# Half-size products with weight sums on GpSimd in block 2's first mixer

## The reference, cut to what matters

```
h = rms_norm_2(x, norm_mix[l]) * (1.0 + sc1) + sh1
proj = h @ w_in[l]
dn_qkv, dn_z, dn_a, dn_b, sw_q, sw_k, sw_v, gate_a, gate_b = split(proj)
o_dn = gated_delta_rule_chunked(dq, dk, dv, g, beta)       # 8 heads of 128, chunks of 64
o_dn = rms_norm_2(o_dn, dn_norm[l]) * silu(dn_z)
y_a = o_dn @ w_dn_out[l]
y_b = swa_sink_attention(sq, sk, sv, swa_sinks[l]) @ w_swa_out[l]   # 16 heads of 64
x = x + gt1 * ((sigmoid(gate_a) * y_a + sigmoid(gate_b) * y_b) @ w_o[l])
```

## Time and profile before

| | us |
|---|---|
| median of three runs | 2584.17 (2582.35 to 2584.47) |
| the profiled execution | 2589.01 |
| its span, first to last instruction | 2587.2 |

### The profile page before, as it was taken

The page is one execution under the profiler, slowest core; times in us unless marked ns, Lnnn a source line. Parts: engine busy times, 40 slices in busy tenths (PEclk is TensorE's granted clock), DMA queues, the critical chain, the costliest instruction groups (busy, mean ns, idle before and its releaser), DMA issues.

```text
span 2587.2 us, 39719 instructions
## 1 busy us (share of the span) xinstructions
PE 2514.9 (97%) x16196; PEld 1938.5 (75%) x16196; DVE 1595.8 (62%) x3137; ACT 654.9 (25%) x1733; POOL 44.7 (2%) x84
## 2 busy tenths in 40 slices
PE   6999899999999999999999999999999999999999
PEld 2545557888888876599996845669997864668999
DVE  4857667655777645466663764447773664447785
ACT  3135422111101112122212153233321134232320
POOL 0000000000000001000000000000000000000000
PEclk9999999999999999999999999999999999999999
DMA  8531215555575758245644423135654333115653
GB/s 338 185 115 27 64 33 164 162 169 173 187 269 187 277 203 308 87 123 155 169 158 148 163 77 120 67 104 146 174 173 143 130 123 105 66 68 151 175 175 119
DMA packets 342646, 386.70 MB, mean 149 GB/s; under 512 B 8110, under 2 KB 285190, under 8 KB 330176
## 3 DMA queue, kind: packets, MB, share of 16 engines
q1 hardware_dynamic: 330896, 320.89, 39.3%
q0 software_dynamic: 8832, 57.26, 6.2%
q10 hardware_dynamic: 2736, 6.01, 0.6%
HBM read 383.08 MB, written 1.05 MB: 148 GB/s over the span
## 4 chain that ended last, share of the span: by engine, by line
PE 84%; DVE 7%; issue 3%; ACT 3%; DMA 3%; ACTq 0%; DVEq 0%; SPq 0%
PE acc L923 32%; PE mx L923 14%; PE acc L974 9%; PE acc L962 9%; PE acc L988 6%; PE acc L1402 2%; PE acc L1351 2%; PE mx L1756 1%; DMA ring<-in_odd_w_in 1%; PE mx L1213 1%; DVE arena L3574 1%; DVE hT L2683 1%; DMA mod_w<-in_w_ada 1%; PE mx L1743 1%; PE mx L1814 1%
## 5 line engine op out<-in xcount | busy, mean ns | idle before, releaser
L923 PE MATMUL acc<-arena 128*128 128x128 f32 (+1 forms) x2248 | 353.8, 300 | 1.0 <-ACT gate L2312 0.5
L923 PEld LDWEIGHTS acc<-arena 128*128 128x128 f32 x2248 | 310.0, 192 | 16.8 <-ACT gate L2312 0.9
L2651 DVE SCALAR_TENSOR_TENSOR arena<-mod_w,vcols,arena 128x2048 f32<-128x2048 f32 x98 | 228.3, 2347 | 59.4 <-DMA mod_w<-in_w_ada 45.2
L974 PE MATMUL acc<-hT,ring 128*128 128x256 f32 (+1 forms) x1024 | 250.0, 406 | 1.3 <-DVE arena L3351 0.8
L988 PE MATMUL acc<-ring,hT 128*128 128x512 f32 x512 | 247.4, 605 | 0.7 <-ACT hT L2095 0.7
L974 PEld LDWEIGHTS acc<-hT,ring 128*128 128x128 f32 x1024 | 193.9, 190 | 54.9 <-issue 29.4
L923 PE MATMUL acc<-hT,ring 128*128 128x128 f32 (+1 forms) x1368 | 206.1, 301 | 2.8 <-ACT hT L2062 1.4
L3027 DVE TENSOR_TENSOR arena<-ring 128x512 f32<-128x512 f32 (+1 forms) x136 | 91.6, 673 | 179.8 <-PE acc L923 174.4
L962 PE MATMUL acc<-ring,hT 128*128 128x512 f32 x448 | 195.5, 597 | 5.9 <-ACT hT L2062 4.6
L923 PEld LDWEIGHTS acc<-hT,ring 128*128 128x128 f32 x1368 | 184.8, 191 | 16.1 <-issue 6.4
L923 PE MATMUL acc<-arena,ring 128*128 128x128 f32 (+1 forms) x1256 | 194.2, 298 | 0.0
(11 more groups left out here) (472 smaller groups left out, 3531.3 us busy)
## 6 DMA issues: line engine op xcount, KB each, us to landing
ring<-in_w_in SPq DMA_DIRECT2D x28, 2048.0 KB
mod_w<-in_w_ada POOLq DMA_DIRECT2D x48, 1024.0 KB, 5.9
ring<-in_ffn_w_in SPq DMA_DIRECT2D x88, 512.0 KB
ring<-in_w_up SPq DMA_DIRECT2D x88, 512.0 KB
mod_w<-in_mod_w SPq DMA_DIRECT2D x36, 1024.0 KB, 4.9
ring<-in_odd_w_in SPq DMA_DIRECT2D x20, 1024.0 KB
ring<-in_ffn_w_out SPq DMA_DIRECT2D x16, 1024.0 KB
ring<-in_w_down SPq DMA_DIRECT2D x16, 1024.0 KB
```

The lines of the kernel that those rows point to most:

```text
L923: ins = nc.tensor.matmul(out, w[:, k, :], h[:, k, :], start=start and k == 0, stop=stop and k == n - 1, skip_group_check=more)
L974: ins = nc.tensor.matmul(b[:, 0:hi - lo], w[:, k, P * f:P * (f + 1)], hT[:, k, lo:hi], start=k == 0, stop=k == KD - 1)
L2651: ins = V.scalar_tensor_tensor(acc_, mod_w[:, i % 2, :], vcols[:, at:at + 1], acc_, ALU.mult, ALU.add)
```

## The change

The four large products of each layer become eight units, one for each weight tile of 512 columns (z, z, attention output twice, gate b twice, gate a twice). A unit is seven products of 128 tokens by 256 columns over 4 blocks of 128, 14 "halves" of two float32 matmuls each; `fill(n)` issues n halves. So a layer has 112 fills where it had 128. `pair_fills` gives one half instead of two at steps 4, 7, 11 and 15. The 8 and 8 fills around the norms become 6 and 6; the one between the two parts of inversion levels 1 to 4 goes; the six at the end of a head group become one ahead of the third ACT copy's wait and five at the end.

POOL computes the four weight sums of every unit (1024 columns each, in SBUF). Each waits for the one before it; the fourth also waits for product 2 of the unit (half 10), whose weights it overwrites, and product 3 (halves 13, 14) waits for the fourth. A ring slot is free when product 3 is done. DVE makes four input sums (512 columns each) for h and for the attention output in each layer, and three additions of 256 columns for each unit. ACT makes four copies of 256 columns for each unit, in place of two of 512.

Two smaller edits: DVE's three instructions for mask, maximum and shift become two `tensor_tensor_reduce`, one for each head, writing the negated scores and their minimum (ACT's exponential gets scale -1). In the first block's recurrence `scores` issues, for each 32 query columns of a chunk, a product with that chunk's 64 keys only, into its half of the partitions: 16 products of 64 x 32 in place of 8 of 128 x 64, for each head and direction.

```diff
+WIDE, HALVES = 8, 14
+WIDE_COPIES, WIDE_SUMS = (("p1", 2), ("u2", 6), ("u3", 9), ("c01", 12)), (("c11", 9), ("c00", 10), ("c10", 14))
 def pair_fills(step):
 
-    return 1 if step in (0, 1, 2, 9, 13, 16, 17) else 2 if step < PAIRS else 0
+    return 1 if step in (0, 1, 2, 4, 7, 9, 11, 13, 15, 16, 17) else 2 if step < PAIRS else 0
...
+            def wide_weights_summed(l, n):
+                u = wide_unit(l, n)
+                c = RV_TILES + WIDE * l + n
+                t = pl.tile[f"wide@{l}"] + 2 * n
+                b = rv_tile(t)
+                t3, t2 = wide_weight_sums(n)
+                if n == 0:
+                    need(pool, merged, 5 * l)
+                elif n == 1:
+                    pool.wait_ge(acc_full, pl.own[f"swa_qkT@{l}"][-1] + 1)
+                elif n == 5:
+                    pool.wait_ge(rv_z, wide_unit(l, 3) + 1)
+                elif n == 6:
+                    pool.wait_ge(rv_z, wide_unit(l, 3) + 1)
+                    pool.wait_ge(rv_p6, wide_unit(l, 5) + 1)
+                else:
+                    pool.wait_ge(rv_p7, u - 1)
+                    if n == 7:
+                        pool.wait_ge(rv_p6, u)
+                pool.wait_ge(w_in[t // 2 % RING], pl.landed[t][1])
+                nc.gpsimd.tensor_tensor(t3, b[0][0], b[0][1], ALU.subtract).then_inc(rv_t, 1)
+                pool.wait_ge(rv_t, 4 * c + 1)
+                nc.gpsimd.tensor_tensor(b[0][1], b[0][1], b[1][1], ALU.add).then_inc(rv_t, 1)
+                pool.wait_ge(rv_t, 4 * c + 2)
+                nc.gpsimd.tensor_tensor(t2, b[0][1], b[0][0], ALU.subtract).then_inc(rv_t, 1)
+                pool.wait_ge(rv_t, 4 * c + 3)
+                pool.wait_ge(rv_p2, u + 1)
+                nc.gpsimd.tensor_tensor(b[1][0], b[1][0], t2, ALU.subtract).then_inc(rv_t, 1)
+            for n in range(WIDE):
+                wide_weights_summed(0, n)
...
+                for n in range(WIDE):
+                    u, c = wide_unit(l, n), RV_TILES + WIDE * l + n
+                    summed_in = 4 * (2 + 2 * l + (n in (2, 3)))
+                    x_ = wide_x(n)
+                    a_, (s1, s2, s3, s4) = wide_inputs(n), wide_input_sums(n)
+                    t3, t2 = wide_weight_sums(n)
+                    if n < 2:
+                        bank_free(n)
+                    else:
+                        pe.wait_ge(rv_c01, u)
+                    first = tile.n
+                    weights(512)
+                    b = rv_tile(first)
+                    half(x_, a_[0][0], b[0][0], 0)
+                    yield
+                    half(x_, a_[0][0], b[0][0], 1).then_inc(rv_p1, 1)
+                    yield
+                    pe.wait_ge(rv_t, 4 * c + 2)
+                    pe.wait_ge(rv_s, summed_in + 1)
+                    if n == 0:
+                        bank_free(2)
+                    else:
+                        pe.wait_ge(rv_c10, u)
+                    half(wide_z, s1, b[0][1], 0)
+                    yield
+                    half(wide_z, s1, b[0][1], 1)
+                    yield
+                    pe.wait_ge(rv_t, 4 * c + 3)
+                    pe.wait_ge(rv_s, summed_in + 3)
+                    pe.wait_ge(rv_p1s, u + 1)
+                    half(x_, s2, t2, 0, first=False)
+                    yield
+                    half(x_, s2, t2, 1, first=False).then_inc(rv_p6, 1)
+                    yield
+                    if n == 0:
+                        bank_free(3)
+                    elif n == 1:
+                        emptied(pl.own[name_of("dn_cum")][0] + 1, "V")
+                    else:
+                        pe.wait_ge(rv_c00, u)
+                    half(wide_p2, a_[0][1], b[1][0], 0)
+                    yield
+                    pe.wait_ge(rv_u2s, u + 1)
+                    half(x_, s3, t3, 0, first=False)
+                    yield
+                    half(x_, s3, t3, 1, first=False).then_inc(rv_p7, 1)
+                    yield
+                    half(wide_p2, a_[0][1], b[1][0], 1).then_inc(rv_p2, 1)
+                    yield
+                    pe.wait_ge(rv_u3s, u + 1)
+                    pe.wait_ge(rv_s, summed_in + 4)
+                    half(x_, s4, b[1][1], 0, first=False)
+                    yield
+                    half(x_, s4, b[1][1], 1, first=False).then_inc(rv_x, 1)
+                    yield
+                    pe.wait_ge(rv_t, 4 * c + 4)
+                    pe.wait_ge(rv_c11, u + 1)
+                    half(wide_z, a_[1][1], b[1][0], 0, first=False)
+                    yield
+                    half(wide_z, a_[1][1], b[1][0], 1, first=False).then_inc(rv_z, 1)
+                    yield
+            def fill(n):
 
                 for _ in range(n):
-                    s = filling.next()
-                    k, i = s % KD, tiles[s // KD % 2]
-                    if s % 16 == 0:
-                        filling.w = weights(512)
-                    if k == 0:
-                        filling.b = bank()
-                    ins = nc.tensor.matmul(filling.b, src[:, k, P * i:P * (i + 1)], filling.w[:, k, :],
-                                           start=k == 0, stop=k == KD - 1)
-                    if k == KD - 1:
-                        ins.then_inc(acc_full, 1)
+                    next(filling.wide)
...
                 for t in range(NT):
-                    s = slice(P * t, P * (t + 1))
                     for early in (True, False):
                         at = 32 * (early == (d == 1))
-                        q = e_set[d][0][:, s].rearrange("p (n t) -> p n t", t=64)[:, :, at:at + 32]
-                        o = hg_bank(h, d, 1)[:, s].rearrange("p (n t) -> p n t", t=64)[:, :, at:at + 32]
-                        ins = nc.tensor.matmul(o, (h_kz[d] if early else e_set[d][1])[:, s], q, start=True, stop=True)
+                        for c in (2 * t, 2 * t + 1):
+                            half, s = slice(64 * (c % 2), 64 * (c % 2) + 64), slice(64 * c, 64 * c + 64)
+                            q = slice(64 * c + at, 64 * c + at + 32)
+                            ins = nc.tensor.matmul(hg_bank(h, d, 1)[half, q], (h_kz[d] if early else e_set[d][1])[:, s],
+                                                   e_set[d][0][:, q], start=True, stop=True)
                 ins.then_inc(hg_s, 1)
...
+                        if name == "p1":
+                            act.wait_ge(rv_p1, u + 1)
+                            act.wait_ge(rv_c00, u)
+                            nc.scalar.activation(wide_p1, wide_x(n), ACT.Copy).then_inc(rv_p1s, 1)
+                        elif name == "u2":
+                            act.wait_ge(rv_p6, u + 1)
+                            act.wait_ge(rv_c10, u)
+                            nc.scalar.activation(wide_u2, wide_x(n), ACT.Copy).then_inc(rv_u2s, 1)
+                        elif name == "u3":
+                            act.wait_ge(rv_p7, u + 1)
+                            act.wait_ge(rv_c11, u)
+                            nc.scalar.activation(wide_u3, wide_x(n), ACT.Copy).then_inc(rv_u3s, 1)
+                        else:
+                            act.wait_ge(rv_x, u + 1)
+                            nc.scalar.activation(wide_out(n, 0, 1), wide_x(n), ACT.Copy).then_inc(rv_c01, 1)
...
                 silu_tanh()
-                act.wait_ge(acc_a, pl.emptied("A", pl.own[name_of("dn_z")][3] + 1))
+                all_wide(2)
...
-                        link(V.scalar_tensor_tensor(S[:, :, 0:w], mx[:, 0:2, 0:w], HD ** -0.5, rep(mask(i), 1, [P, 2, w]),
-                                                    ALU.mult, ALU.add))
-                        link(V.reduce_max(st[:, 40 + c:42 + c], S[:, :, 0:w], AXX))
-                        V.scalar_tensor_tensor(st[:, 8 + c:10 + c], st[:, 40 + c:42 + c], -1.0, less[:, j, :],
-                                               ALU.mult, ALU.min).then_inc(att_m, 1)
+                        for v in range(2):
+                            ins = V.tensor_tensor_reduce(S[:, v, 0:w], mx[:, v, 0:w], mask(i), -HD ** -0.5, less[:, j, v:v + 1],
+                                                         ALU.add, ALU.min, st[:, 8 + c + v:9 + c + v])
+                        ins.then_inc(att_m, 1)
...
+                def wide_inputs_summed(n):
+                    (a00, a01), (a10, a11) = wide_inputs(n)
+                    s1, s2, s3, s4 = wide_input_sums(n)
+                    s0 = 4 * (2 + 2 * l + (n in (2, 3)))
+                    V.tensor_tensor(s1, a10, a00, ALU.subtract).then_inc(rv_s, 1)
+                    V.tensor_tensor(s3, a11, a10, ALU.subtract).then_inc(rv_s, 1)
+                    dve.wait_ge(rv_s, s0 + 1)
+                    V.tensor_tensor(s2, a11, s1, ALU.subtract).then_inc(rv_s, 1)
+                    dve.wait_ge(rv_s, s0 + 3)
+                    V.tensor_tensor(s4, a01, s2, ALU.subtract).then_inc(rv_s, 1)
+                halves_done = Cursor()
+                def wide_done(n):
+                    lo = halves_done.n
+                    halves_done.n += n
```

(69 more changed lines are left out.)

152 lines of the change are left out of this document (97 added, 55 removed).

## The result

| | us |
|---|---|
| changed kernel, median of four runs | 2651.7 (2647.1 to 2662.3) |
| kernel before, on the same chip | 2583.3 (2580.7 to 2584.5) |
| ratio | 1.0271, 95% interval 1.0251 to 1.029 |

The change makes the kernel 68 us slower. The forecast was 2569, its range ended at 2618, and its likeliest case had the wrong sign.

The account below looks back on a forecast made before the run. TensorE was taken as the bound, busy for 97% of the span, with DVE never far behind. Gains of 36.2 us less losses of 21.0 gave 15.2 off, so 2569 us; own range 2562 to 2577, full range 2557 to 2618.

Parts of the forecast that it names:

- part 5: POOL's weight sums: 2.5 us each, exposed after the norms and at two hand-overs, costing 8.6 us a layer.
- rival A: POOL's sums and DVE's two-SBUF-operand or double-rate instructions wait for each other: 77 us lost, 2625 us; chance 0.33.
- Part 1: Large products: 112 groups of four 256-column matmuls at 1.73 us replace 219.6 us of fill products; gain 25.8 us.
- Part 2: Inversion levels 1 to 4 lose their fills, gain 2.1 us; final products' wait for ACT's third copy covered, gain 2.8.
- Parts 3 and 4: Attention's mask in two DVE instructions for three, gain 1.0 us; chunked scores, 1.15 us per group for 1.73, gain 4.5.
- Parts 5 and 6: POOL's sums cost 8.6 us a layer; ACT's copies queued in order cost 1.5 after the attention, 0.4 elsewhere, a layer.

Follow-up runs that it names:

- the kernel where nothing is awaited: Changed kernel, but POOL's 64 instructions read two different operands on buffers nobody reads and PE waits for them only a unit later: 2654.1 us.
- eight pauses: Kernel before with chunked scores and fused mask, PE made to wait for 150 one-column POOL constants after each chunk's second transposes: 2614.7 us.

## Why the prediction was wrong

**The step that failed is the choice between part 5 and rival A.** Part 5 priced a sum at 2.5 us and asked who waits for its result. The size was right, 2.37 to 2.80 us by its kinds, 2.50 on average; and the waits that it asked for stayed small, 3.6 us of PE for POOL in a layer. The question was wrong: it isn't POOL's result that is awaited, but DVE, whose instructions stand behind POOL's. Rival A said that, named its instructions (L3538, L3539, the small sums and the normalisations are among the stretched rows) and priced it at 77 us; it got 0.33, and "nothing in this trace" was the argument against. The absence of rows was taken for evidence against a mechanism that these rows could not have shown. Measured, it is 85 us: 85.3 between the changed kernel and the one without sums, 88 in the kernel where nothing is awaited.

The Trainium skill (SBUF — State Buffer, "Who interferes with whom") sets two conditions, reading on both sides, or a DVE in a 2-port mode against any use by GpSimd, and full blocking in place of sharing. The traces agree: 0.69 us stays 0.69 beside constants and becomes 2.84 beside sums, and the copy is held by both. The ratio of two against DVE in its GPSIMD Engine Reference, "Elementwise — side-by-side cycle accounting", holds too: 2.37 us, the shortest kind of sum, against 1.22 is 1.9. The longest kind, 2.80, is 2.3 times.

**Rival A's own working** put 39 us on a layer. The account against the kernel without sums is 40.4 us in the first layer: 26.9 of idle time (38.2 - 11.3), 10.4 of low clock, and 3 more of PE's busy time that I have not traced. It had no term for the clock, and the idle part is 26.9 where it had 39. It expected attention and norms to cost 6 of 39, so 15 in 100; they cost 40. The waits above show the place: L2908, the attention's normalisation, holds up PE for 6.5 us and L3711 for 3.8, 10.3 together where it had 6.

**Part 1, the columns: right.** The halves come 0.216 us per 256 columns: four in 0.86 us in these two rows, as the earlier trace rows.

```profile
1597.76 1.03 PE L1074 MATMUL acc<-x,gate 128*128 128x256 f32 x4
...
1598.62 1.02 PE L1985 MATMUL mx<-arena,fconst 128*128 128x512 f32 x2
```

448 of them are 96.9 us, against 109.8 for the fills: 12.9 a layer. The kernel without sums has 12.5 us less busy time of PE in the first mixer than the one with the two small parts (195.90 above against this row's 208.40):

```profile
1481.90:1696.40 214.50, 208.40 (x1906) 120.94 (x1904) 99.25 (x333) 87.90 (x261) 2.43 (x5) 1.00 0.27 82
```

**Part 2, the moved fills: half right.** The wait of the final products for ACT's copy is gone from PE's waits, as forecast. But "nothing that the fill hid comes out" failed. Without sums two levels of the first head group take longer than the 2.42 of the earlier trace rows, 3.21 (below) and 3.07:

```profile
1596.86 0.27 PE L2016 MATMUL mx<-arena 64*64 64x64 f32 x1
...
1600.07 0.22 PE L2016 MATMUL mx<-arena 64*64 64x64 f32 x1
```

Over the first layer the levels 1 to 4 of both groups take some 2 us more than eight times 2.42. The forecast gain of 1.05 a layer turned into a loss of about 1. PE's waits there are put down to issue, 0.8 at the longest; what comes late isn't settled.

**Parts 3 and 4: right as a sum.** The mask gives 1.3 us in a mixer by its trace (215.8 to 214.5), with L2722's wait gone, and 1.5 in all by the medians; the forecast had 1.0 in all. A group of scores went from 1.73 to 1.06 us from its first start to the next instruction's (forecast 1.15). Eight times 0.67 is 5.4, of which the run of the scores alone returns 1.8, at most 4.6 by its interval. Both together gave 5.5, the forecast's number; that the terms are each right isn't shown.

**Parts 5 and 6 without POOL.** ACT's copy after the attention costs 1.4 us, as forecast (1.5). The hand-overs, though, remain when there are no sums at all: 2.3 us at the second transposes (L1990) and 2.1 at the end of the mixer (L1272), where the kernel before had 0.9 and nothing, besides 1.0 at the levels. I had priced them at 3.3 and 3.5 a layer with product 3's wait for the fourth sum in them. Without that wait about half of it remains, 1.4 and 2.1 us more than before, and that half is the order itself: in the trace without sums c10 is made only when PE has finished product 3, 0.95 us after DVE is ready for it, and z's four products follow behind it (1625.77 to 1628.77 us). The seven products keep 7.3 us in the first layer (214.5 to 207.2): 12.5 gained in busy time and 5.2 returned in idle time (6.1 to 11.3).

**The sum.** Without POOL 32.4 were forecast and 16.8 measured; losses by POOL of 17.2 (8.6 a layer) were forecast and 85 measured. The second number decides the sign, and would have done so with every gain in full.

## What to carry to other kernels

Before an idle engine is given work, look at what it shares with the busy one. If GpSimd is to read SBUF beside a DVE that is busy for half of the time or more (here 107 of the mixer's 216 us, 68% of its dense stretches), count each of its instructions as an instruction of DVE's own for those that have two SBUF operands or copy at double rate, and put it at the head of what DVE does next. A mechanism that is stated precisely and whose conditions the new code meets isn't made unlikely by an old trace that could have no row of it; here it was what happened. And when waits of some 3 us come into a stretch that PE filled without gaps, price the low clock that may follow them beside the idle time itself.

## What was not expected of the hardware

- How sharp the limit is: 57 us of POOL's constants in the mixer cost 1.3 to 2 us a layer, 77 us of its reading sums 43. Each constant is also shorter than a sum, 0.95 us against 2.5, and how much of the difference that makes isn't shown. A DVE instruction of 0.16 us (L2900, the small sum of the attention) was stretched to 1.45 us beside a sum.
- The loss grows faster than the length of POOL's instruction: 48 us at 2.04 us, 88 at 2.48; and 39 us came back by cutting each in two, though POOL was then busy for longer.
- PE's clock fell to 1.2 GHz in a mixer that was otherwise at 2.4 GHz: ten times in the two mixers of the changed kernel, around the end of idle stretches of 2.0 to 4.7 us, and five times behind eight pauses of 3.4 us. It doesn't follow every one; what decides isn't settled here. It made up a quarter of the loss in the mixer, and a quarter of a pause's price.
- One-column constants on POOL in a row come 34 ns apart (416 in 14.2 us), though the record of each lasts 98 ns.
